# Hybrid encoder block: in the expert stage, the two prompt batches of a pair of phases stand together ahead of the pair's sample units, and there are twelve raw weight slots

## What is computed

```python
def _expert_choice_ffn(h, w_router, w_e_gate, w_e_up, w_e_down):
    cap = CAPACITY_FACTOR * T // N_EXPERTS          # 32 prompt rows, 128 sample rows per expert
    aff = jax.nn.softmax((ht @ w_router).astype(jnp.float32), axis=-1)
    gate_vals, idx = lax.top_k(aff.T, cap)
    xe = ht[idx]
    hid = jax.nn.silu(jnp.einsum('ecd,edf->ecf', xe, w_e_gate)) * jnp.einsum('ecd,edf->ecf', xe, w_e_up)
    ye = jnp.einsum('ecf,efd->ecd', hid, w_e_down) * gate_vals[..., None].astype(h.dtype)
    out = jnp.zeros((T, D), ye.dtype).at[idx.reshape(-1)].add(ye.reshape(-1, D))
```

## Time and profile before

| | us |
|---|---|
| median of 3 runs | 3150.28 (3149.73 to 3151.01) |
| span of the profiled execution | 3149.8 |
| PE busy | 3021.8 (96%) |
| weight loads on PE busy | 2391.6 (76%) |
| DVE busy | 1715.3 (54%) |
| ACT busy | 1521.5 (48%) |
| GpSimd busy | 560.9 (18%) |

### The profile page before, as it was taken

One profiled execution on the slowest core, in us unless ns is written; L12 is line 12 of the kernel. 1 busy time (PEld: TensorE's weight loads), 2 busy tenths in 40 slices (PEclk: granted clock), 3 DMA queues, 4 the chain that ended last, 5 costly groups with the idle time before them and its releaser, 6 DMA issues. The chain is left out here.

```text
span 3149.8 us, 51649 instructions
## 1 busy us (share of the span) xinstructions
PE 3021.8 (96%) x19370; PEld 2391.6 (76%) x19370; DVE 1715.3 (54%) x1748; ACT 1521.5 (48%) x1659; POOL 560.9 (18%) x729
## 2 busy tenths in 40 slices
PE   8999999999989999999949999999999999999998
PEld 6888886777778799878837777777777777777776
DVE  4101000555443599924367676666667676666665
ACT  4211111455632366622435665655666665556554
POOL 0048883112220000011100111000111100111100
PEclk9999999999999999999969999999999999999999
DMA  5224323233335100063447887778888778888874
GB/s 184 105 99 143 121 90 103 96 111 115 95 111 195 55 20 20 7 227 135 160 163 260 296 285 273 276 284 293 293 296 293 270 274 299 284 289 291 293 273 146
DMA packets 196414, 600.32 MB, mean 191 GB/s; under 512 B 15392, under 2 KB 45744, under 8 KB 196336
## 3 DMA queue, kind: packets, MB, share of 16 engines
q1 hardware_dynamic: 166144, 508.03, 44.9%
q0 software_dynamic: 21328, 73.41, 7.8%
q10 hardware_dynamic: 8864, 17.83, 1.6%
HBM read 521.80 MB, written 77.33 MB: 190 GB/s over the span
## 5 line engine op out<-in xcount | busy, mean ns | idle before, releaser
L2069 DVE TENSOR_TENSOR ex_w_lo<-ex_w_raw,ex_w_hi 128x2048 fp32r<-128x2048 f32 x384 | 880.0, 2292 | 451.1 <-ACT ex_w_hi L2024 451.1
L2024 ACT ACTIVATE ex_w_hi<-ex_w_raw 128x2048 fp32r<-128x2048 f32 x381 | 729.9, 1916 | 469.6 <-PE ex_ps_s L2156 469.5
L2156 PE MATMUL ex_ps_s<-ex_w_hi,ex_xS 128*128 128x512 f32 x2048 | 578.5, 396 | 0.0
L2156 PEld LDWEIGHTS ex_ps_s<-ex_w_hi,ex_xS 128*128 128x128 f32 x2048 | 376.2, 188 | 99.1 <-issue 26.3
L2156 PE MATMUL ex_ps_s<-ex_w_lo,ex_xS 128*128 128x512 f32 x1024 | 316.7, 390 | 0.0
L2156 PE MATMUL ex_ps_s<-ex_w_hi,ex_hidS 128*128 128x512 f32 x1024 | 308.1, 403 | 0.0
L2010 POOL DMA_INDIRECT y<-ex_ye_s,ex_rows_y x16 | 43.7, 2729 | 1147.1 <-DVE ex_ye_s L2112 1147.1
L2167 PE MATMUL ex_ps_p<-ex_w_raw,ex_xP 128*32 128x256 f32 x4096 | 236.1, 383 | 0.0
L2156 PEld LDWEIGHTS ex_ps_s<-ex_w_lo,ex_xS 128*128 128x128 f32 x1024 | 192.4, 188 | 41.3
L109 PE MATMUL pj_ps_tok<-pj_w_hi,act_hl 128*128 128x512 f32 x560 | 219.9, 393 | 2.4 <-DVE act_hl L436 2.4
L111 PE MATMUL pj_ps_tok<-pj_w_hi,act_hl 128*128 128x512 f32 x560 | 218.9, 391 | 0.0
(11 more groups left out here) (334 smaller groups left out, 5140.1 us busy)
## 6 DMA issues: line engine op xcount, KB each, us to landing
ex_w_raw<-w_e_gate SPq DMA_DIRECT2D x128, 1024.0 KB, 11.3
ex_w_raw<-w_e_up SPq DMA_DIRECT2D x128, 1024.0 KB, 11.7
ex_w_raw<-w_e_down SPq DMA_DIRECT2D x128, 1024.0 KB, 8.7
proj_t<-pj_stage SPq DMA_DIRECT2D x60, 256.0 KB, 2.1
pj_w_raw<-w_cols ACTq DMA_DIRECT2D x7, 2048.0 KB, 8.8
z_w_raw<-w_z SPq DMA_DIRECT2D x16, 512.0 KB, 4.0
gate_logits<-gl_z_stage SPq DMA_DIRECT2D x32, 256.0 KB, 2.1
pj_w_raw<-x SPq DMA_DIRECT2D x10, 512.0 KB, 3.7
```

Of the source, the lines that this page charges most:

```text
L2024: act.activation(whl[0][:, j % NHL], raw[:, j % NRAW], ACT.Copy).then_inc(w_hi, 1)
L2069: dve.tensor_tensor(whl[1][:, j % NHL], raw[:, j % NRAW], whl[0][:, j % NHL].bitcast(F32), ALU.subtract).then_inc(w_lo, 1)
L2156: mm = pe.matmul(ps_s[:, s, c:c + 512], x(part, k), whl[w][:, j % NHL, kk, c:c + 512], start=k == 0 and part + w == 0, stop=k == 2 * PU - ...
```

## The change

Four things, all in the expert stage:

- **PE:** at the head of a pair (units 0, 8 and 16) both prompt batches of the pair stand one behind the other, and the pair's eight sample units follow without a break. The turns of the hidden prompt part move from after units 8 and 16 to after units 4 and 12 (`P_TURN`); those of the sample part stay after units 9 and 10, 17 and 18 (`S_TURN` = 9 and 17). DVE's product of the prompt part moves from its steps 4, 12 and 20 to 2, 10 and 18, and its copies of the turned prompt part from 9 and 17 to 5 and 13.
- **Slots:** `NRAW` is 12, and `start_weights` loads all twelve within `choose`.
- **Buffers:** the silu is written into the hidden tile itself (`silu_s` and `silu_p` are gone), with waits of ACT for the earlier turns. The sample's hidden and output tiles lie in one tensor, `late`, that first holds `affT`, `vals`, `lists` and `idx`.
- **Phase 4's head** waits for `turn_out` q+4 (both turned prompt parts) ahead of its two batches. The waits of phase 4's and phase 5's first units for q+3 and q+6 are as before.

```diff
-        NRAW, NHL, LEAD = 8, 4, 3
+        NRAW, NHL, LEAD = 12, 4, 3
+        P_TURN, S_TURN = (4, 12), (9, 17)
...
-        sgS, sgP = ph.sb("silu_s", [CS, HF]), ph.sb("silu_p", [P, QW])
-        hS, hP = ph.sb("hidden_s", [CS, HF]), ph.sb("hidden_p", [P, QW])
-        yS, yP = ph.sb("ye_s", [CS, D]), ph.sb("ye_p", [P, QW])
+        hS, yS = late[:, 0:HF], late[:, HF:HF + D]
+        hP, yP = ph.sb("hidden_p", [P, QW]), ph.sb("ye_p", [P, QW])
...
-                sp.dma_start(raw[:, j], gu_d[f][:, 0:1, k, 0:HF].rearrange("p e k c -> p (e k) c")).then_inc(w_in[j], 16)
+                sp.dma_start(raw[:, j], gu_d[f % 2][:, 0:1, k, f // 2 * HF:(f // 2 + 1) * HF].rearrange("p e k c -> p (e k) c")).then_inc(w_in[j], 16)
...
-                        sp.wait_ge(p_full, CR + PHASES * e + f - 1)
+                        sp.wait_ge(p_full, CR + PHASES * e + f - NRAW // PU + 1)
...
-                        for f, at in ((0, 10), (1, 18)):
+                        for f, at in enumerate(S_TURN):
                             for r in range(2):
-                                if j == at + r:
+                                if j == at + 1 + r:
                                     turn_high(e, 3 * f + r + 1, hidS[:, 0, f * FC + 4 * r:f * FC + 4 * r + 4], (3 * f + r + 1) % 2)
...
-                                act.activation(sgS[:], ps_s[:, 0], ACT.Silu).then_inc(act_s, 1)
+                                act.wait_ge(turned, CR + XT + TURNS * e + (3 if f == 2 else 6 - TURNS))
+                                act.activation(hS, ps_s[:, 0], ACT.Silu).then_inc(act_s, 1)
...
-                        for f, at in ((0, 9), (1, 17)):
-                            if j == at:
+                        for f, at in enumerate(S_TURN):
+                            if j == P_TURN[f] + 1:
                                 dve.wait_ge(turned, CR + q + 3 * f + 1)
...
-                        if f % 2 == 1 and j % PU == 0:
-                            dve.wait_ge(p_full, CR + PHASES * e + f + 1)
+                        if j % (2 * PU) == 2:
+                            dve.wait_ge(p_full, CR + PHASES * e + f + 2)
                             dve.wait_ge(act_p, CR + 3 * e + f // 2 + 1)
...
-                        if i == 0:
-                            pe.wait_ge((act_p, dve_p)[f % 2], CR + 3 * e + f // 2)
+                        if i == 0 and f % 2 == 0:
                             if f == 0:
                                 pe.wait_ge(turn_out, CR + q - 2)
-                            if f >= 4:
-                                pe.wait_ge(turn_out, CR + q + 3 * (f - 4) + 1)
-                                prompt(e, f, lambda k, c: hidP[:, f - 4, k % 2, CP * (k // 2):CP * (k // 2) + CP])
-                            else:
-                                prompt(e, f, lambda k, c: xP[:, k])
+                            if f == 4:
+                                pe.wait_ge(turn_out, CR + q + 4)
+                            for b, evacuated in enumerate((act_p, dve_p)):
+                                pe.wait_ge(evacuated, CR + 3 * e + f // 2)
+                                if f == 4:
+                                    prompt(e, f + b, lambda k, c: hidP[:, b, k % 2, CP * (k // 2):CP * (k // 2) + CP])
+                                else:
+                                    prompt(e, f + b, lambda k, c: xP[:, k])
+                        if i == 0:
                             pe.wait_ge((act_s, dve_s)[f % 2], CR + 3 * e + f // 2)
...
-                        for g, at in ((0, 8), (1, 16)):
-                            if at <= j < at + 3:
-                                r = j - at
+                        for g, at in enumerate(S_TURN):
+                            if j in (P_TURN[g], at, at + 1):
+                                r = 0 if j == P_TURN[g] else j - at + 1
...
+            late = router.enter_context(nc.sbuf_tensor("choice_then_rows", [P, T + TS // 2 + 5 * CS], F32))
```

More of the change, by code:

```diff
@@ L1909, in choose, with experts @@
         ph.clear()
-def experts(nc, affT, vals, lists, idx, h2, y, w_gate, w_up, w_down, slots_i, slots_g, slots_q, cst):
+def experts(nc, late, affT, vals, lists, idx, h2, y, w_gate, w_up, w_down, slots_i, slots_g, slots_q, cst):
     with ExitStack() as ctx:
@@ L2008, in body @@
                     ph.settle(pool)
-                    for j, (dst, src) in enumerate(((y, yS), (y_q, yP))):
-                        pool.indirect_dma_start(dst, bass.IndirectOffsetOnAxis(ap=rows_y[j][:, 0:1], axis=0), src[:], None,
+                    for j, (dst, src) in enumerate(((y, yS), (y_q, yP[:]))):
+                        pool.indirect_dma_start(dst, bass.IndirectOffsetOnAxis(ap=rows_y[j][:, 0:1], axis=0), src, None,
                                                 compute_op=ALU.add).then_inc(scattered[j], 16)
@@ L2046, in body @@
                             if f < 4:
-                                act.activation(sgP[:], ps_p[:, 0, 0:QW], ACT.Silu).then_inc(act_p, 1)
+                                act.wait_ge(turned, CR + XT + TURNS * e + (1 if f == 2 else 4 - TURNS))
+                                act.activation(hP[:], ps_p[:, 0, 0:QW], ACT.Silu).then_inc(act_p, 1)
                             else:
@@ L2054, in body @@
                             if f < 4:
-                                act.activation(sgS[:], ps_s[:, 0], ACT.Silu).then_inc(act_s, 1)
+                                act.wait_ge(turned, CR + XT + TURNS * e + (3 if f == 2 else 6 - TURNS))
+                                act.activation(hS, ps_s[:, 0], ACT.Silu).then_inc(act_s, 1)
                             else:
-                                act.activation(yS[:], ps_s[:, 0], ACT.Copy, scale=gate[0][:]).then_inc(act_s, 1)
+                                act.activation(yS, ps_s[:, 0], ACT.Copy, scale=gate[0][:]).then_inc(act_s, 1)
                 for r in range(2):
@@ L2108, in body @@
                             if f < 4:
[L2109 to L2110 removed]
+                                dve.tensor_tensor(hS, hS, ps_s[:, 1], ALU.mult).then_inc(dve_s, 1)
                             else:
[L2112 removed]
+                                dve.scalar_tensor_tensor(out=yS, in0=ps_s[:, 1], scalar=gate[0][:], in1=yS,
                                                          op0=ALU.mult, op1=ALU.add).then_inc(dve_s, 1)
@@ L2272, in program @@
         with ExitStack() as router:
[L2273 to L2276, removed]
+            late = router.enter_context(nc.sbuf_tensor("choice_then_rows", [P, T + TS // 2 + 5 * CS], F32))
+            at_lists = T + TS // 2
+            affT, vals = late[0:NE, 0:T], late[0:ROWS, T:at_lists]
+            lists = late[0:ROWS, at_lists:at_lists + 4 * CS].rearrange("p (j c) -> p j c", j=4)
+            idx = late[0:ROWS, at_lists + 4 * CS:at_lists + 5 * CS].bitcast(U32)
             with shared_rows, out_stage:
                 finish_mixer(nc, dram["x"], merged, w_out_raw, w_out_in, first_parts, first_tile, merged_stored, dram["norm_ffn"], dram["w_router"], cst, dram["y"], h2, affT, vals, lists, idx)
-            experts(nc, affT, vals, lists, idx, h2, dram["y"], dram["w_e_gate"], dram["w_e_up"], dram["w_e_down"], slots_i, slots_g, slots_q, cst)
+            experts(nc, late, affT, vals, lists, idx, h2, dram["y"], dram["w_e_gate"], dram["w_e_up"], dram["w_e_down"], slots_i, slots_g, slots_q, cst)
 W_IN_ORDER = [(3104, 4128), (4128, 4640), (1024, 2048), (2048, 3072), (0, 1024), (3072, 3088), (3072, 3088), (3088, 3104)]
```

3 lines of the change are left out of this document (1 added, 2 removed).

## The result

| | before | after |
|---|---|---|
| median, us | 3150.01 (3149.23 to 3151.01, 4 runs) | 3193.28 (3192.84 to 3193.80, 4 runs) |
| span of the profiled execution, us | 3149.8 | 3191.3 |

The ratio is 1.0135, with a 95% interval of 1.0124 to 1.0147. The forecast was 3171.5 us (3160 to 3186): the direction was right, the size was not. The kernel loses 43 us where 21 were forecast.

What follows compares the result with a forecast made beforehand. PE's instruction stream from expert 0's gather on was taken as the bound. 3149.8 - 17.4 (seams) + 33.1 (stall) + 5.5 (start) = 3171.0, plus 0.5 from span to median: 3171.5 us, range 3160 to 3186.

Steps and rivals of the forecast that it cites:

- The seams: Tile-form changes around PE's prompt batches: pairing saves one 0.36 us return trip a pair, 17.4 us in all; batch-to-batch seam 0.
- a pair of plain phases without turns: Sign in the profile after: such a pair takes 29.04 us, its two batches 7.2 us from first to last.
- The stall: PE at unit 20 waits for DVE's second copy of pair 1's turned sample rows: 2.07 us per expert, 33.1 in all.
- DVE's moved product: Output's prompt-part product, moved from DVE step 20 to 18 ahead of the late copy, adds 0.06 us to the stall.
- from DVE's end to PE's start: Small stall term at unit 20: PE starts 0.05 us after DVE's late copy ends.
- The clock: Rival: the granted clock falls at the unit 20 stalls, 1.7 us each; 3180 or 3199 us; chance 0.10.
- one fall in three: Clock rival's partial case: a fall at one expert in three costs 9 us, giving 3180 us.
- the full case: Clock rival with the clock falling at all experts' stalls: 3199 us.
- two gaps: Like PE gaps of 2.09 us before the change: one left the clock at 1.00, after the other it was 0.66 over 5 us.
- The start: Twelve loads instead of eight within `choose` delay expert 0's gather, for which PE waits, by 5.5 us (bounds 0 and 6.6).
- An equal share between the queues: Alternative for the start: the gather is late by only about 1.6 us, making the sum 3167.
- Weights and other waits: PE's other expert-stage waits stay covered: 3.7 us to spare on weight splits, next need for loads over 25 us away.

Runs made afterwards that it cites:

- the late wait last: Changed kernel with PE's wait for q+6 put behind unit 20's other waits, directly ahead of its matmuls; 3171.85 us, 1.0067 of the kernel before.

## Why the prediction was wrong, step by step

**The seams: right.** 0.36 us a pair, and nothing between two batches, were forecast; 1.08 us per expert (17.3 us in all, against 17.4) and 7.04 us for two batches were measured. The Trainium skill's rule that a change of the tiling mode drains the engine ("TensorEngine Tiling (Array Packing)", Key Properties) agrees with both. The sign that the forecast named for it, a pair of plain phases without turns, does not exist: after the change each pair has turns. The period without a wait, 91.35 us, takes its place.

**The stall: place, cause and main term right, one small term mis-sized.** The copy is late by 1835.27 - 1833.43 = 1.84 us, as forecast to the hundredth. DVE's moved product costs nothing (0.06 forecast): from turn to copy's end it is 5.04 us with and without it. The step that failed is "from DVE's end to PE's start", taken as 0.05 us from the earlier trace rows: it was 0.32, since in the earlier trace rows no satisfied waits stand behind the late one. Expert by expert the stall is 93.63 - 91.35 = 2.28 us instead of 2.07, 3.4 us over 16 and beyond its upper bound of 2.2.

**The clock: wrong, and this is most of the miss.** The forecast had the mechanism and its price (1.7 us, against 1.6), but as a rival at 0.10 with one fall in three, and its range ended below the full case. The sentence that failed is "The new gap is a little shorter and has dense work on both sides". A gap of the 1.73 us that follow from a term of 0.05 does hold the clock, in 30 of 30 cases; the real one, 2.00 us, was practically the 2.09 of the earlier trace rows, and dense work on both sides was no protection. The forecast's two gaps were three, with one fall, so its "one expert in three" was a fair reading; the 12 of 16 hung on the waits' moments, which no row of before gives. So one mis-sized term of 0.27 us carried the second error: with the late wait last, which restores that term, the period is 93.40 us and the time 3171.85, where 93.4 and 3171.5 had been forecast. That the medians agree to 0.4 us is partly luck: its runs range from 3169.14 to 3172.88.

**The start: right in size.** 5.5 us were forecast (bounds 0 and 6.6). The gather's wait grew from 8.72 to 13.44 us, 4.7, and undoing it gave back 4.8. In the direct comparison of the two spans only 3.04 us appear, because the choice of rows ended 1.68 us earlier in this execution. An equal share between the queues, as the Trainium skill's page "DMA: Bandwidth & Descriptors" (Queues, rings and completion order) can be read, would have given the estimate of 1.6 us; the measurement speaks against that reading, as the earlier trace rows did. In this kernel the gather was issued at 1647.98 us, while the twelve loads still ran:

```profile
1640.00:1650.00 10.00, 0.90 (x4) 0.61 (x4) 3.25 (x18) 0.00 (x0) 2.21 (x4) 0.50 1.03 409
1650.00:1657.00 7.00, 0.54 (x6) 0.57 (x6) 0.00 (x0) 0.00 (x0) 0.00 (x0) 0.50 1.01 361
```

DMA is busy throughout until PE's start at 1656.46, at 409 and 361 GB/s, as foreseen.

**The sum, corrected.** 21.2 us forecast on the span, + 19.2 for the clock, + 3.4 for the stall, - 2.5 for the start (3.04 instead of 5.5) is 41.3, against 41.5 measured.

**Weights and other waits: right.** No other wait of PE from the experts appears in the list of waits.

## What to carry to other kernels

When work that stands between two steps is moved away, look for the wait that it used to cover, and work out by how much its producer is late; here that showed the loss ahead of time, and one step of `S_TURN` turns it into a gain. A repeated idle gap on TensorE has to be priced twice, by its length and by the granted clock behind it; where the trace of before has gaps of about that length with both outcomes, the case in which the clock falls at most of them belongs inside the range. In a loop, put the wait that comes last behind those that are long satisfied.

## What was not expected of the hardware

- Idle gaps of 1.73 us on TensorE left the granted clock at 1.00 in 30 of 30 cases; gaps of 2.00 us, with dense matmuls on both sides, brought it to 1.2 GHz in 22 of 30, at 1.6 us each, in a pattern that follows the moment of the gap and not only its length.
- Inside a loop, three satisfied semaphore waits behind the one that PE is held by delay its next matmul by 0.26 us (0.32 from DVE's end to PE's start, against 0.06).
- Four MB of loads more in flight delay an indirect gather by 4.7 us.
